# Expert down matrices issued from ScalarE's queue at the begin of their step

## The chip, the cores and the metric

The kernel runs on one core of a Trainium2 chip. The time is the device time of one execution in microseconds (us). The core's engines are TensorE (PE in the profile; its weight loads PEld), VectorE (DVE), ScalarE (ACT), GpSimd (POOL) and SyncE (SP), each with its own stream of instructions; they meet through semaphores. Transfers between memory and the on-chip buffers run on 16 DMA engines and are issued from the streams of SyncE, ScalarE and GpSimd.

## The reference

One layer of an encoder block on 512 tokens of width 1024, in float32: a projection, spatial gating and stick-breaking attention, an output product with layer norm, then a mixture of 64 routed experts (8 per token) with one shared expert, an embedding gate and a last layer norm. The change concerns the experts alone. Of the reference, this is what matters:

```python
def expert_block(args):
    tok, e = args
    xb = x_pad[tok]
    hb = jax.nn.silu(xb @ w_gate[e]) * (xb @ w_up[e])
    return hb @ w_down[e]
yb = lax.map(expert_block, ...)
routed = jax.ops.segment_sum(yb * row_w[:, None], row_tok, ...)
```

w_gate[e] and w_up[e] are 1024 x 256, w_down[e] is 256 x 1024: three matrices of 1 MB for each expert, 192 MB in all.

## The kernel before, in words

The stages follow one another: the dense part (`mix_stage`, `out_stage`), the experts (`experts_stage`), and the embedding gate with the last norm (`Embedding`). The span of the experts' loop is from about 412 to 1028 us.

All products of the experts keep float32 accuracy with three matmuls: each operand is split into a high part (rounded to fp32r by ScalarE) and a low part (the rest, by VectorE), and `product3` (lines 414 to 416) computes hi*hi, lo*hi and hi*lo. So each weight matrix that lands in a raw buffer is read once by ScalarE, which writes the high part, and once by VectorE, which writes the low part.

The work on one expert x is spread over steps. There are 64 steps, written out by hand for every engine as `step(x)`; `all_experts` unrolls the first four and the last eight, and runs the others as a hardware loop of four steps a pass. In step x:

- TensorE turns h of expert x-1 (`turn_h`, line 1532), locates the tokens of x+4 (line 1499), multiplies gate and up of x (24 matmuls of 512 columns), turns the gathered rows of x+1 (line 1508), and multiplies down of x-1 (12 matmuls).
- ScalarE copies the high part of h of x-1 (hT_hi, line 1622), the high parts of gate and up of x+1 (w_hi, line 1603, twice), between them scales the result of x-2 (y, line 1637) and writes an index list (put_idx, line 1629), then silu of x (line 1618), the high part of the rows of x+1 (xgT_hi, line 1613), and the high part of down of x (dn_hi, line 1609).
- VectorE does the low parts in the same order: hT_lo (line 1739), w_lo twice (line 1718), found and get_idx and the one-hot tiles of later experts between them, h_ff = silu * up (line 1734), xgT_lo (line 1728) and dn_lo (line 1723).
- GpSimd gathers the rows of x+4 (line 1821) and scatters those of x-1 with an add (line 1833).
- SyncE loads the weights. `load_down(x)` (line 1464) waits until VectorE has split the down matrix of x-2, which frees one of two raw buffers, dn_raw. `load_gate_up(x+2)` (line 451, once for each half) waits until the low parts of x are written, which frees one of four buffers, gu_raw. SyncE has no other work in the loop, so it runs ahead of the step that ScalarE and VectorE are in, as far as these waits let it.

The first and the last step differ. In step 0 ScalarE has only put_idx, dn_hi, silu and xgT_hi to do, dn_hi standing before silu. In the last step (`at == -1`) there is nothing left to split of gate and up, and dn_hi stands before silu on ScalarE and dn_lo before h_ff on VectorE. After its last step SyncE issues the loads of the embedding stage: p_rows (line 1906), p_w (line 1907) and two pieces of ple_raw (line 380).

Two lines carry the synchronisation of the down matrix on ScalarE:

```python
act.wait_ge(dn_in[x.b], 16 * x.turn2)          # the load has landed
act.wait_ge(y_sum, x.it - 2 + 1 + LEAD)        # the product of x-2 is done
```

Of the kernel before, what the change touches and what calls it, by code (L numbers as in the profile page):

```python
# [17 lines left out]
P = 128  # L18
# [1113 lines left out]
class Routing:  # L1132
# [32 lines left out]
    def load_down(self, sp):  # L1165
        sp.dma_start(self.m.sh_down[:], self.a["sh_w_down"][0].rearrange("(p j) n -> p (j n)", p=P)) \
          .then_inc(self.down_in, 16)
# [224 lines left out]
def experts_stage(nc, m, ps, stack, a, h1, acc_dram, acc_odd_dram, CAP, early, routing, embedding):  # L1392
# [7 lines left out]
    LEAD = 2  # L1400
# [4 lines left out]
    w_down = a["moe_w_down"][0]  # L1405
    def sem(name):
        return stack.enter_context(nc.semaphore(f"moe_{name}"))

    gu_in, put, cleared = early.gu_in, early.put, early.cleared
    dn_in = [sem(f"dn_in{b}") for b in range(2)]  # L1410
    gu_hi, gu_lo = sem("gu_hi"), sem("gu_lo")
    dn_hi, dn_lo = sem("dn_hi"), sem("dn_lo")
# [12 lines left out]
    def rounds(eng, body, finish=None):  # L1425

        eng.wait_ge(routing.peak_ready, 1)
        peak[0] = eng.value_load(m.peak_i[0:1, 0:1], min_val=0, max_val=SEQ)
        body(0, True)
        if finish is not None:  # L1430
            with eng.If(peak[0] <= CAP):
                finish(eng)
        with eng.If(peak[0] > CAP):
            with eng.Fori(1, ROUNDS) as r:
                with eng.If(peak[0] > r * CAP):
                    body(r, False)
            if finish is not None:
                finish(eng)

    def all_experts(eng, r, step):  # L1440

        for q in range(4):
            step(Expert(r, 0, q), q)
        with eng.Fori(1, QUADS - 2) as quad:
            for q in range(4):
                step(Expert(r, quad, q))
        for quad in (QUADS - 2, QUADS - 1):
            for q in range(4):
                step(Expert(r, quad, q), 4 * (quad - QUADS) + q)

    def x_banks():

        return ps[:, XT:XT + 2, 0:4 * CAP]

    def sync(sp):
        def load_gate_up(x):
            for half in range(2):

                sp.wait_ge(gu_lo, 2 * x.it + half - 4 + 1 + 2 * LEAD)
                early.load_half(sp, x, half)  # L1460

        def load_down(x):
            sp.wait_ge(dn_lo, x.it - 2 + 1 + LEAD)
            sp.dma_start(m.dn_raw[:, x.b:x.b + 1],
                         w_down[bass.ds(x.e, 1)].rearrange("o (p j) n -> p o (j n)", p=P)) \
              .then_inc(dn_in[x.b], 16)

        def body(r, first):
            if not first:
                for q in range(3):  # L1470
                    load_gate_up(Expert(r, 0, q))

            def step(x, at=99):
                load_down(x)
                if at not in (0, -1, -2):
                    load_gate_up(x.next(2))

            all_experts(sp, r, step)
            with sp.If(peak[0] <= (r + 1) * CAP):
                sp.wait_ge(gu_lo, 2 * ((r + 1) * NE) + 2 * LEAD)  # L1480
                embedding.load_p(sp)
                embedding.load_weights(sp, 0)

        load_gate_up(Expert(0, 0, 2))
        rounds(sp, body)
        embedding.sync(sp)
# [111 lines left out]
    def scalar(act):  # L1598
        def split(x, half):
            act.wait_ge(gu_in[x.b][half], 16 * x.turn2)  # L1600
            if half == 0:
                act.wait_ge(gu_sum, x.it - 2 + 1 + LEAD)
            nc.scalar.activation(m.w_hi[:, 2 * x.b + half], m.gu_raw[:, 2 * x.b + half],  # L1603
                                 ACT.Copy).then_inc(gu_hi, 1)

        def split_down(x):
            act.wait_ge(dn_in[x.b], 16 * x.turn2)
            act.wait_ge(y_sum, x.it - 2 + 1 + LEAD)
            nc.scalar.activation(m.dn_hi[:, x.b], m.dn_raw[:, x.b], ACT.Copy).then_inc(dn_hi, 1)  # L1609

        def split_x(x):
            act.wait_ge(x_turned, x.it + 1 + LEAD4)
            nc.scalar.activation(m.xgT_hi[:, x.b].rearrange("p (c n) -> p c n", c=2), x_banks(),  # L1613
                                 ACT.Copy).then_inc(x_hi, 1)

        def silu(x):
            act.wait_ge(gu_sum, x.it + 1 + LEAD)
            nc.scalar.activation(m.silu[0:CAP, x.b], ps[0:CAP, GU[x.b], 0:FF], ACT.Silu).then_inc(silu_out, 1)

        def split_hT(x):  # L1620
            act.wait_ge(h_turned, x.it + 1)
            nc.scalar.activation(m.hT_hi[:, x.b], ps[:, HT, 0:2 * CAP], ACT.Copy).then_inc(hT_hi, 1)

        def put_list(x, at=99):

            if at not in (0, 2):
                act.wait_ge(put[x.b], 16 * (x.turn2 - 2 + ZEROS[x.b]))
            act.wait_ge(found, x.it + 1 + LEAD)
            nc.scalar.activation(m.put_idx[x.q][0:CAP],  # L1629
                                 m.found[0:CAP, bass.ds(x.e, 1), 0:1].rearrange("p o c -> p (o c)"),  # L1630
                                 ACT.Identity, bias=m.far[0:CAP]).then_inc(put_ready, 1)

        def scale_y(x, bank=Y):

            act.wait_ge(y_sum, x.it + 1 + LEAD)
            act.wait_ge(put[x.b], 16 * (x.turn2 - 1 + ZEROS[x.b]))
            nc.scalar.activation(m.y[x.b][0:CAP].rearrange("p (c n) -> p c n", n=512), ps[0:CAP, bank:bank + 2],
                                 ACT.Copy,
                                 scale=m.found[0:CAP, bass.ds(x.e, 1), 1:2].rearrange("p o c -> p (o c)")) \
              .then_inc(y_ready, 1)  # L1640

        def body(r, first):
            if not first:
                for q in range(2):
                    split(Expert(r, 0, q), 0)
                    split(Expert(r, 0, q), 1)
                split_x(Expert(r, 0, 0))

            def step(x, at=99):
                if at != 0:  # L1650
                    split_hT(x.next(-1))
                if at not in (0, -1):
                    split(x.next(1), 0)
                if at not in (0, 1):
                    scale_y(x.next(-2))
                put_list(x, at if first else 99)
                if at not in (0, -1):
                    split(x.next(1), 1)
                if at in (0, -1):
                    split_down(x)  # L1660
                silu(x)
                if at != -1:
                    split_x(x.next(1))
                if at not in (0, -1):
                    split_down(x)
                if at == -1:
                    split_hT(x)
                    scale_y(x.next(-1))

            all_experts(act, r, step)  # L1670
            scale_y(Expert(r, QUADS - 1, 3), bank=XT)

        act.sem_inc(y_ready, LEAD)
        split(Expert(0, 0, 0), 0)
        routing.silu(act, 0)
        split(Expert(0, 0, 0), 1)
        routing.silu(act, 1)
        routing.sigmoid(act)
        routing.silu(act, 2)
        routing.silu(act, 3)  # L1680
        routing.copy_hT(act, 0)
        routing.copy_hT(act, 1)
        split(Expert(0, 0, 1), 0)
        split(Expert(0, 0, 1), 1)
        routing.copy_hT(act, 2)
        routing.copy_hT(act, 3)
        routing.store_rows(act, 0)
        routing.store_rows(act, 1)
        split_x(Expert(0, 0, 0))
        routing.store_rows(act, 2)  # L1690
        routing.store_rows(act, 3)
        rounds(act, body, embedding.scalar_weights)
        embedding.scalar(act)
# [119 lines left out]
    def gpsimd(pool):  # L1813
# [50 lines left out]
        embedding.gpsimd(pool)  # L1864

    return Stage(sync, tensor, scalar, vector, gpsimd, prime)


# [286 lines left out]
```

## Time and profile before

| | us |
|---|---|
| median of 3 runs | 1108.08 |
| lowest, highest | 1106.89, 1109.62 |
| profiled execution | 1109.13 |
| span of its trace | 1107.4 |
| TensorE, VectorE, ScalarE busy | 1069.6, 864.8, 713.8 |
| mean granted TensorE clock | 0.993 |

How to read it: the span is from the first to the last instruction of the core. Busy time is the time in which at least one instruction of the engine runs; a matmul's end is modelled and overlaps the next one's start, so that the distance between starts is the better measure of TensorE's rate. A row of the timeline begins with the start and the length in us; a bracket at its end gives the idle time of the engine before it and what ended it. SPq and ACTq are the sequencers of SyncE and ScalarE, which issue DMAs while the engine itself is not counted as busy. The DMA share is the time that packets took divided by 16 engines.

### The profile page before, as it was taken

What the parts mean: (1) busy time and instruction counts of PE and PEld (TensorE: products, weight loads), DVE (VectorE), ACT (ScalarE), POOL (GpSimd) and SP (SyncE); (2) the same over time, 40 slices, a digit from 0 to 9 for tenths busy, and PEclk for the clock granted to TensorE, in tenths of its full rate; (3) what the DMA queues carried; (4) which work ended last, traced back from release to release, by engine and by line L of the source; (5) the groups of instructions that cost most, each with busy time, mean ns of one, the idle gap of its engine ahead of it and who ended that gap; (6) DMA issues with size and microseconds to landing.
All of it is one profiled execution on the core that took longest, in us unless ns stands there. A gap on an engine that the chain in (4) does not pass through costs nothing.

```text
span 1107.4 us, 15674 instructions
## 1 busy us (share of the span) xinstructions
PE 1069.6 (97%) x5374; PEld 871.6 (79%) x5374; DVE 864.8 (78%) x966; ACT 713.8 (64%) x761; POOL 298.9 (27%) x173
## 2 busy tenths in 40 slices
PE   4999999999999989999999999999999999999986
PEld 3878877778888747888888888888888888888575
DVE  6654345662365687999999999999999999998366
ACT  3431235452143426888888888888888888888643
POOL 1000000000004023444444444444444444432101
PEclk9999999999999999999999999999999999999999
DMA  9432221113365357999999999999999999998811
GB/s 328 153 117 76 76 77 59 57 47 143 114 239 211 132 204 265 362 389 384 386 376 379 383 386 391 390 387 379 379 380 374 377 389 386 388 388 279 288 71 59
DMA packets 72573, 294.81 MB, mean 266 GB/s; under 512 B 15313, under 2 KB 18385, under 8 KB 47697
## 3 DMA queue, kind: packets, MB, share of 16 engines
q1 hardware_dynamic: 52944, 256.43, 59.1%
q0 software_dynamic: 19008, 35.71, 12.6%
q10 hardware_dynamic: 576, 2.10, 0.5%
q8 instruction: 26, 0.43, 0.2%
q14 instruction: 19, 0.15, 0.0%
HBM read 283.67 MB, written 44.04 MB: 296 GB/s over the span
## 4 chain that ended last, share of the span: by engine, by line
PE 88%; DVE 6%; DMA 3%; issue 1%; ACT 1%; SPq 0%; DVEq 0%; POOLq 0%; ACTq 0%
PE ps L414 26%; PE ps L416 25%; PE ps L415 25%; PE ps L1508 5%; PE ps L1532 1%; DVE w_lo L398 1%; PE ps L729 1%; PE ps L753 1%; DMA x_odd<-odd_rows 1%; PE ps L740 1%; DMA xg<-h_rows,get_idx 1%; DMA ln_b<-in_ln_in_b 1%; DVE x_rows L310 0%; PE ps L1499 0%; PE ps L323 0%
## 5 line engine op out<-in xcount | busy, mean ns | idle before, releaser
L1718 DVE TENSOR_TENSOR w_lo<-gu_raw,w_hi 128x2048 fp32r<-128x2048 f32 x128 | 292.2, 2283 | 3.3 <-ACT w_hi L1603 3.3
L1603 ACT ACTIVATE w_hi<-gu_raw 128x2048 fp32r<-128x2048 f32 x128 | 244.8, 1913 | 0.0
L414 PE MATMUL ps<-w_hi,xgT_hi 128*128 128x512 f32 x512 | 206.6, 404 | 4.1 <-issue 4.1
L416 PE MATMUL ps<-w_hi,xgT_lo 128*128 128x512 f32 x512 | 201.6, 394 | 0.0
L415 PE MATMUL ps<-w_lo,xgT_hi 128*128 128x512 f32 x512 | 200.9, 392 | 0.0
L1821 POOL DMA_INDIRECT xg<-h_rows,get_idx x64 | 143.2, 2237 | 74.8 <-DVE get_idx L1712 55.1
L414 PE MATMUL ps<-w_hi,act_hi 128*128 128x512 f32 x384 | 155.3, 404 | 5.2 <-DVE act_lo L2035 3.6
L1723 DVE TENSOR_TENSOR dn_lo<-dn_raw,dn_hi 128x2048 fp32r<-128x2048 f32 x64 | 146.7, 2292 | 8.4 <-ACT dn_hi L1609 4.8
L416 PE MATMUL ps<-w_hi,act_lo 128*128 128x512 f32 x384 | 151.4, 394 | 0.0
L415 PE MATMUL ps<-w_lo,act_hi 128*128 128x512 f32 x384 | 151.3, 394 | 0.0
L1609 ACT ACTIVATE dn_hi<-dn_raw 128x2048 fp32r<-128x2048 f32 x64 | 122.1, 1908 | 0.0
L293 POOL TENSOR_TENSOR x_rows<-x_rows,ln_b 128x1024 f32<-128x1024 f32 x6 | 14.8, 2459 | 392.0 <-DVE x_rows L286 392.0
L414 PEld LDWEIGHTS ps<-w_hi,xgT_hi 128*128 128x128 f32 x512 | 96.9, 189 | 22.8 <-issue 4.2
L416 PEld LDWEIGHTS ps<-w_hi,xgT_lo 128*128 128x128 f32 x512 | 96.9, 189 | 20.9
L415 PEld LDWEIGHTS ps<-w_lo,xgT_hi 128*128 128x128 f32 x512 | 97.1, 190 | 18.5
L1833 POOL DMA_INDIRECT residual_rows<-y,put_idx x32 | 64.6, 2018 | 162.8 <-ACT put_idx L1629 88.8
L414 PE MATMUL ps<-dn_hi,hT_hi 128*128 128x512 f32 x256 | 105.4, 412 | 0.0
L1833 POOL DMA_INDIRECT odd_rows<-y,put_idx x32 | 62.6, 1957 | 157.9 <-ACT put_idx L1629 156.7
L416 PE MATMUL ps<-dn_hi,hT_lo 128*128 128x512 f32 x256 | 101.0, 395 | 0.0
L415 PE MATMUL ps<-dn_lo,hT_hi 128*128 128x512 f32 x256 | 100.2, 391 | 0.0
L393 ACT ACTIVATE w_hi<-raw 128x2048 fp32r<-128x2048 f32 x28 | 53.4, 1915 | 64.0 <-PE ps L416 48.1
L1613 ACT ACTIVATE xgT_hi<-ps 128x1024 fp32r<-128x1024 f32 x64 | 65.8, 1029 | 41.3 <-PE ps L1508 41.3
(198 smaller groups left out, 1738.3 us busy)
## 6 DMA issues: line engine op xcount, KB each, us to landing
gu_raw<-in_moe_w_gate SPq DMA_DIRECT2D x64, 1024.0 KB, 10.1
gu_raw<-in_moe_w_up SPq DMA_DIRECT2D x64, 1024.0 KB, 9.9
dn_raw<-in_moe_w_down SPq DMA_DIRECT2D x64, 1024.0 KB, 9.1
raw<-in_w_in SPq DMA_DIRECT2D x18, 1024.0 KB, 5.1
h_rows<-x_rows SPq DMA_DIRECT2D x8, 512.0 KB, 5.0
raw<-in_w_out SPq DMA_DIRECT2D x4, 1024.0 KB, 5.0
ple_raw<-in_ple_w_gate SPq DMA_DIRECT2D x4, 1024.0 KB, 10.9
x_rows<-in_x SPq DMA_DIRECT2D x4, 512.0 KB, 9.9
```

The lines of the kernel that those rows point to most:

```text
L393: self.nc.scalar.activation(self.m.w_hi[:, i % NSPLIT], self.raw[i % self.slots], ACT.Copy).then_inc(self.hi_split, 1)
L414: nc.tensor.matmul(out, x_hi, w_hi, start=first, stop=False)
L415: nc.tensor.matmul(out, x_hi, w_lo, start=False, stop=False)
L416: return nc.tensor.matmul(out, x_lo, w_hi, start=False, stop=last)
L1508: last = nc.tensor.transpose(ps[:, XT + k // 4, (k % 4) * CAP:(k % 4 + 1) * CAP], m.xg[x.q][0:CAP, k::KD], m.ident[0:CAP, 0:CAP])
L1603: nc.scalar.activation(m.w_hi[:, 2 * x.b + half], m.gu_raw[:, 2 * x.b + half], ACT.Copy).then_inc(gu_hi, 1)
L1609: nc.scalar.activation(m.dn_hi[:, x.b], m.dn_raw[:, x.b], ACT.Copy).then_inc(dn_hi, 1)
L1613: nc.scalar.activation(m.xgT_hi[:, x.b].rearrange("p (c n) -> p c n", c=2), x_banks(), ACT.Copy).then_inc(x_hi, 1)
L1718: nc.vector.tensor_tensor(m.w_lo[:, 2 * x.b + half], m.gu_raw[:, 2 * x.b + half], m.w_hi[:, 2 * x.b + half].bitcast(F32), ALU.subtract).th ...
L1723: nc.vector.tensor_tensor(m.dn_lo[:, x.b], m.dn_raw[:, x.b], m.dn_hi[:, x.b].bitcast(F32), ALU.subtract).then_inc(dn_lo, 1)
L1821: nc.gpsimd.indirect_dma_start(out=m.xg[x.q][0:CAP], out_offset=None, in_=h1, in_offset=bass.IndirectOffsetOnAxis(ap=m.get_idx[x.q][0:CAP] ...
L1833: nc.gpsimd.indirect_dma_start(out=(acc_dram, acc_odd_dram)[x.b], out_offset=bass.IndirectOffsetOnAxis(ap=m.put_idx[x.q][0:CAP], axis=0), ...
```

## The change

The function `load_down` moves from SyncE's stream to ScalarE's, with the same wait, the same transfer and the same semaphores. SyncE's step is left with the gate and up loads. On ScalarE the load stands at the begin of step x, behind hT_hi of x-1 and before the first split of gate and up of x+1.

```diff
-        def load_down(x):
-            sp.wait_ge(dn_lo, x.it - 2 + 1 + LEAD)
-            sp.dma_start(m.dn_raw[:, x.b:x.b + 1],
-                         w_down[bass.ds(x.e, 1)].rearrange("o (p j) n -> p o (j n)", p=P)) \
-              .then_inc(dn_in[x.b], 16)
-
...
             def step(x, at=99):
-                load_down(x)
                 if at not in (0, -1, -2):
                     load_gate_up(x.next(2))
...
+        def load_down(x):
+            act.wait_ge(dn_lo, x.it - 2 + 1 + LEAD)
+            act.dma_start(m.dn_raw[:, x.b:x.b + 1],
+                          w_down[bass.ds(x.e, 1)].rearrange("o (p j) n -> p o (j n)", p=P)) \
+               .then_inc(dn_in[x.b], 16)
+
...
             def step(x, at=99):
                 if at != 0:
                     split_hT(x.next(-1))
+                load_down(x)
                 if at not in (0, -1):
                     split(x.next(1), 0)
```

ScalarE, an unrolled step (x = 3) of the kernel before; dn_raw is the raw down matrix, dn_hi its high part, w_hi that of gate or up, ps is PSUM:

```order
L1622 ACTIVATE hT_hi<-ps 128x256 [waits moe_h_turned]
L1603 ACTIVATE w_hi<-gu_raw 128x2048 [waits moe_gu_sum,moe_gu_in00]
L1637 ACTIVATE y_138<-ps,found 128x1024 [waits moe_put_odd,moe_y_sum]
L1629 ACTIVATE put_idx_122<-found,far 128x1 [waits moe_found,moe_put_odd]
L1603 ACTIVATE w_hi<-gu_raw 128x2048 [waits moe_gu_in01]
L1618 ACTIVATE silu<-ps 128x256 [waits moe_gu_sum]
L1613 ACTIVATE xgT_hi<-ps 128x1024 [waits moe_x_turned]
L1609 ACTIVATE dn_hi<-dn_raw 128x2048 [waits moe_y_sum,moe_dn_in1]
```

The same step of the changed kernel (its line numbers from here on are lower by one on ScalarE and by seven above it):

```order
L1621 ACTIVATE hT_hi<-ps 128x256 [waits moe_h_turned]
L1601 DMA dn_raw<-in_moe_w_down 128x2048 [waits moe_dn_lo]
L1596 ACTIVATE w_hi<-gu_raw 128x2048 [waits moe_gu_sum,moe_gu_in00]
L1636 ACTIVATE y_138<-ps,found 128x1024 [waits moe_put_odd,moe_y_sum]
L1628 ACTIVATE put_idx_122<-found,far 128x1 [waits moe_found,moe_put_odd]
L1596 ACTIVATE w_hi<-gu_raw 128x2048 [waits moe_gu_in01]
L1617 ACTIVATE silu<-ps 128x256 [waits moe_gu_sum]
L1612 ACTIVATE xgT_hi<-ps 128x1024 [waits moe_x_turned]
L1608 ACTIVATE dn_hi<-dn_raw 128x2048 [waits moe_y_sum,moe_dn_in1]
```

The load stands seven instructions ahead of the dn_hi that reads it, both in one step.

ScalarE at the begin of the loop, step 0, in the changed kernel:

```order
L1428 TENSOR_LOAD peak_i [waits route_peak_ready]
L1428 ISA x2
L1601 DMA dn_raw<-in_moe_w_down 128x2048 [waits moe_dn_lo]
L1628 ACTIVATE put_idx_119<-found,far 128x1 [waits moe_found]
L1608 ACTIVATE dn_hi<-dn_raw 128x2048 [waits moe_y_sum,moe_dn_in0]
L1617 ACTIVATE silu<-ps 128x256 [waits moe_gu_sum]
L1612 ACTIVATE xgT_hi<-ps 128x1024 [waits moe_x_turned]
```

Only put_idx stands between the load and its reader, and silu and xgT_hi stand behind the reader.

ScalarE in the last step, in the changed kernel:

```order
L1621 ACTIVATE hT_hi<-ps 128x256 [waits moe_h_turned]
L1601 DMA dn_raw<-in_moe_w_down 128x2048 [waits moe_dn_lo]
L1636 ACTIVATE y_138<-ps,found 128x1024 [waits moe_put_odd,moe_y_sum]
L1628 ACTIVATE put_idx_122<-found,far 128x1 [waits moe_found,moe_put_odd]
L1608 ACTIVATE dn_hi<-dn_raw 128x2048 [waits moe_y_sum,moe_dn_in1]
L1617 ACTIVATE silu<-ps 128x256 [waits moe_gu_sum]
```

Here y and put_idx stand between the load and its reader.

## Rows read from the trace of the kernel before

**Rows 1.** The page: engines' busy time, and DMA busy tenths in 40 slices.
```profile
PE 1069.6 (97%) x5374; PEld 871.6 (79%) x5374; DVE 864.8 (78%) x966; ACT 713.8 (64%) x761; POOL 298.9 (27%) x173
...
DMA  9432221113365357999999999999999999998811
```

**Rows 2.** Windows: PE, PEld, DVE, ACT, POOL busy (x), PEclk, DMA share, GB/s.
```profile
600.00:650.00 50.00, 50.00 (x261) 42.19 (x261) 48.98 (x49) 44.04 (x43) 22.92 (x11) 1.00 1.02 386
```

**Rows 3.** Timeline of ScalarE in one step: start, us, engine, line, operation.
```profile
702.10 0.39 ACT L1622 ACTIVATE hT_hi<-ps 128x256 fp32r<-128x256 f32 x1 [0.17 <-PE ps L1532]
702.38 1.91 ACT L1603 ACTIVATE w_hi<-gu_raw 128x2048 fp32r<-128x2048 f32 x1
...
707.78 0.38 ACT L1618 ACTIVATE silu<-ps 128x256 f32<-128x256 f32 x1 [0.50 <-PE ps L416]
...
709.60 1.91 ACT L1609 ACTIVATE dn_hi<-dn_raw 128x2048 fp32r<-128x2048 f32 x1
```

**Rows 4.** Timeline of SyncE in the same step.
```profile
700.39 0.33 SPq L451 DMA_DIRECT2D gu_raw<-in_moe_w_up  x1
704.28 0.33 SPq L1464 DMA_DIRECT2D dn_raw<-in_moe_w_down  x1
```

**Rows 5.** Timeline of TensorE and VectorE in the same step and the next's begin.
```profile
702.00 0.48 PE L414 MATMUL ps<-w_hi,xgT_hi 128*128 128x512 f32 x1
...
704.51 2.28 DVE L1718 TENSOR_TENSOR w_lo<-gu_raw,w_hi 128x2048 fp32r<-128x2048 f32 x1
...
710.15 1.22 DVE L1728 TENSOR_TENSOR xgT_lo<-ps,xgT_hi 128x1024 fp32r<-128x1024 f32 x1
...
711.54 2.29 DVE L1723 TENSOR_TENSOR dn_lo<-dn_raw,dn_hi 128x2048 fp32r<-128x2048 f32 x1 [0.17 <-ACT dn_hi L1609]
...
711.58 0.47 PE L414 MATMUL ps<-w_hi,xgT_hi 128*128 128x512 f32 x1
```

**Rows 6.** Line 1464: landings of the down loads issued at 425, 465, 580, 963.
```profile
DMA to landing us min/median/max: 4.7/4.7/4.7
...
DMA to landing us min/median/max: 8.1/8.1/8.1
...
DMA to landing us min/median/max: 6.5/6.5/6.5
...
DMA to landing us min/median/max: 12.6/12.6/12.6
```

**Rows 7.** Line 1821: landings of gathers issued at 413, 560 to 580, 950 to 980.
```profile
DMA to landing us min/median/max: 4.5/4.5/4.5
...
DMA to landing us min/median/max: 10.3/10.4/10.5
...
DMA to landing us min/median/max: 10.5/11.0/12.4
```

**Rows 8.** Begin of the loop: ScalarE's timeline, and TensorE's waits (us, times, longest).
```profile
415.74 1.90 ACT L1609 ACTIVATE dn_hi<-dn_raw 128x2048 fp32r<-128x2048 f32 x1
419.78 0.39 ACT L1618 ACTIVATE silu<-ps 128x256 f32<-128x256 f32 x1 [2.15 <-PE ps L416]
420.66 1.02 ACT L1613 ACTIVATE xgT_hi<-ps 128x1024 fp32r<-128x1024 f32 x1 [0.49 <-PE ps L1508]
...
PE ps L414 <- issue: 4.1, 2, 2.3
...
PE ps L1508 <- DMA xg<-h_rows,get_idx: 0.5, 1, 0.5
```

**Rows 9.** End of the loop: timelines of ScalarE, VectorE and SyncE.
```profile
1017.08 0.39 ACT L1622 ACTIVATE hT_hi<-ps 128x256 fp32r<-128x256 f32 x1 [0.17 <-PE ps L1532]
...
1020.49 2.29 DVE L1723 TENSOR_TENSOR dn_lo<-dn_raw,dn_hi 128x2048 fp32r<-128x2048 f32 x1 [0.91 <-ACT dn_hi L1609]
1022.98 0.42 DVE L1734 TENSOR_TENSOR h_ff<-silu,ps 128x256 f32<-128x256 f32 x1 [0.20 <-ACT silu L1618]
...
1015.25 0.38 SPq L1906 DMA_DIRECT2D p_rows<-in_p  x1
```

## The prediction

> **What bounds the kernel now.** I read the page first. TensorE is busy for 97% of the span and VectorE for 78%; the row of the DMA engines shows nines from the fifteenth slice to the thirty-eighth, and that stretch is the experts' stage [rows 1]. Ask next what a window inside it shows: in 50 us TensorE is busy for 50.00, VectorE for 48.98, ScalarE for 44.04, and the DMA share is 1.02 [rows 2]. So three things are full at once there: the matmuls, VectorE and the DMA engines. The timeline of one step says what the period is: the first gate/up matmul stands at 702.00 and the next step's at 711.58, 9.58 us a step without a gap between [rows 5]. Nothing that becomes earlier can shorten such a step; anything that becomes later by more than its slack lengthens it. The reader is to look, then, for slack on three chains: ScalarE to VectorE to TensorE within a step, the landing of the down matrix, and the two ends of the loop, where steps look different.
>
> **What moves.** SyncE issued the down load of expert x as soon as VectorE had split that of x-2, which is nearly a step ahead: the issue at 704.28 [rows 4] is for the next step's expert, whose conversion on ScalarE comes 9.58 us after the one at 709.60 [rows 3], at about 719.2. That is 14.9 us of time to land. Now ScalarE issues it behind hT_hi of its own step (702.10, [rows 3]), so at about 702.3, and the conversion of the same expert is at 709.60. That leaves 7.3 us. The load is the same 1 MB; SyncE's queue loses a third of its loads.
>
> **Term 1, the begin of the loop.** In step 0 the issue stands directly ahead of put_idx and dn_hi. Before, dn_hi ran at 415.74 since its data had long landed [rows 8]. Now the load starts at about 415.4, ahead of put_idx, which takes some 0.3. A down load with idle engines took 4.7 us, and one with other loads about it took 8.1 [rows 6]; here one more gate/up load and two gathers are under way, and I take 6.2, so it lands at 421.6. dn_hi then ends at 423.5 (1.91 us each). Behind it in ScalarE's order stand silu (0.39 us, before at 419.78) and xgT_hi (before at 420.66), and TensorE's second step waits for the latter by way of VectorE [rows 8]. xgT_hi now starts at about 423.8, 3.1 us late. On the other side two loads of 1 MB are gone from ahead of the first gather, but TensorE waited only 0.5 us for that gather [rows 8], so no more than 0.5 comes back. The term is +2.6; with 4.7 it is +1.1, with 8.1 it is +4.5.
>
> **Term 2, the end of the loop.** In the last step dn_hi stands ahead of silu, since no gate/up split is left. The load is issued behind hT_hi at 1017.08, at about 1017.2, and SyncE has put four loads of the next stage in front from 1015.25 on, on the other queue [rows 9]. With 4.7 us it lands at 1021.9, with 8.1 at 1025.3; I take 6.8 and 1024.0. Then come dn_hi (1.91) and on VectorE dn_lo (2.29), which stands ahead of h_ff. Before, dn_lo was through by 1022.78 and h_ff ran at 1022.98, released by silu [rows 9]. Now h_ff can't start before 1024.0 + 1.91 + 2.29 = 1028.2. That is +5.2, and turning h, the down product, the scatter and the next stage all follow from it, so it goes to the end in full. The ends are +3.1 and +6.5.
>
> **Term 3, the issue itself.** SyncE's issue took 0.33 us [rows 4]; with the address arithmetic I take 0.4 on ScalarE. It stands between hT_hi and the first w_hi (702.38), so that w_hi ends at 704.69 instead of 704.29 and w_lo, at 704.51 before, starts at 704.72: +0.2. From w_lo on VectorE runs without a gap to xgT_lo, which ends at 711.37, against TensorE's start at 711.58 [rows 5]. So 0.2 of slack meets 0.2 of delay: I count 0.05 for each of 60 steps, 3 us. ScalarE has the room (0.50 idle before silu [rows 3]), so the second w_hi's delay is nearly covered, and dn_hi isn't moved at all. If the issue were hidden wholly in the shadow of hT_hi the cost is 0; if all 0.4 shows behind the slack, it is 0.2 a step, 12 us.
>
> **Term 4, landing within 7.3 us.** Landing times of the down loads rise from 4.7 on idle engines to 8.1 at 465, fall to 6.5 at 580, and rise to 12.6 at 963 [rows 6]. That is a queue filling slowly: the DMA engines need a trace more than a step for a step's bytes, and the 14.9 us of slack pay for it. With 7.3 us they can't. Put the new slack in the old queue's terms: a load issued at 704.28 that must be there at 709.60 may take 5.3. If the engines are the limit from there on, all of 12.6 - 5.3 = 7.3 us must be spent in waiting somewhere in the loop, once, not in each step, because every wait lets the queue drain. A step that is already longer by term 3 drains it as well, so the two don't add up: 7.3 with 3 beside it I count as 9 together, the ends being 0 and 48 (below). VectorE has 0.17 idle before dn_lo [rows 5], so a late dn_hi reaches TensorE almost whole.
>
> The nearest rows for a load on another queue are the gathers of GpSimd's: 4.5 us on idle engines, 10.4 at 565, 11.0 at 950 to 980 [rows 7], while the loads of SyncE's queue went from 6.5 to 12.6. So a queue beside the full one pays some 6 us for the company, but it doesn't stand behind the whole backlog. A gather's time includes GpSimd's own work on it, so I take it as an upper bound for the down load.
>
> **The rule on this.** The Trainium skill ("DMA: Bandwidth & Descriptors", section "Queues, rings and completion order") says that each DMA engine goes round the queues that have work and drains one packet of descriptors from one before it turns to the next. By that rule a down load on its own queue would wait for what is being served and no more, and the loop would cost nothing; the gathers' level times agree with it. This is the second rival. The section "Issuing engines are not separate DMA queues" of that page says that all issuers share the same 16 engines, which speaks against any gain in bandwidth; the share of 1.02 agrees.
>
> **The sum.** 2.6 + 5.2 + 9 = 16.8 us. The profiled execution took 1109.13 (span 1107.4), 1.05 over the median of the runs shown, 1108.08. 1108.08 + 16.8 = 1124.9; I say 1125.
>
> **The rivals.**
> - *The load is late in every step.* Each landing takes about the 8.1 of row 465 although the queue drains, because ScalarE's load always meets the second gate/up half, issued at 700.39, 1.9 us before it [rows 4], and the gathers. Then 0.8 us in each of 60 steps, 48 us, with terms 1 and 2: 1108 + 56 = 1164. For it: the 8.1 and the gathers' 10.4. Against it: 6.5 at 580 under the same load, and a longer step makes room, which brings the landing towards 4.7. 15%, from 1133 to 1165.
> - *The load is hidden in the loop.* Served beside the backlog it lands in under 7.3 us; what is left is terms 1 to 3: 1108 + 7.8 + 0 to 3 = 1117. For it: the gathers' times don't follow the backlog. Against it: their level is high. 20%, from 1112 to 1120.
> - *Faster.* The first gather and the first steps gain from the lighter queue while the waits at both ends are covered. TensorE's idle time there is 0.5 before the first gather's transposes and 4.1 before the first matmuls of the first two steps [rows 8], so the most it gives is 4.6: 1103.5. It decides only if the loads of steps 0 and 63 land before their conversions are due, 0.3 us and 1.3 us after the issue, where 4.7 is the shortest seen. 4%.
> - *No difference.* Terms 1 and 2 at their lower ends (4.2 us) less what other idle time swallows: 5%.
>
> The forecast itself, all three terms with waits that spend the backlog once, has 56%, with 1120 to 1133 as its own range. Another mean clock is an uncertainty upward: TensorE's granted clock was 0.993 over the span, so part of it ran at the lower level, and longer pauses at the ends may add to that; I don't price it. Below 1112 I leave 9% and above 1146 some 9%. What a measurement of this kernel can tell from no change is about 0.3%, 3.3 us. Slower by more than that: 56 + 15 + 20 = 91%; within it 5%; faster 4%.
>
> **What would show it.** In the new trace dn_hi of step 0 should start near 421.6 and idle time on ScalarE before it should be put down to the load; in the last step dn_hi should stand some 5 us late and h_ff behind it. In the loop, ScalarE's first w_hi should start about 0.7 behind hT_hi instead of 0.28. Waits of dn_hi for the load should appear in many steps, small (0.1 to 1 us) and in sum 5 to 10 us, with landings of down loads near 7.3, and the DMA share still at 1. No waits in the loop would mean the second rival; waits of equal size in all steps and a DMA share clearly under 1 the first. I am wrong if the sum over the two ends is under 4 us, or if TensorE's period in the middle is still 9.58 with the down load landing late, which would mean slack on VectorE that I haven't seen.

## The result, and the profile after

| | before | after |
|---|---|---|
| median, us | 1108.36 (1106.89 to 1109.62, 4 runs) | 1180.96 (1178.98 to 1182.84, 4 runs) |
| ratio | | 1.0655, 95% interval 1.0632 to 1.0678 |
| span of the profiled execution, us | 1107.4 | 1181.1 |
| granted clock over the span | 0.993 | 0.984 |

The kernel is 6.5% slower. The forecast was 1125 us with a range up to 1146: the sign was right, the size four times too small. I place the difference first by the starts of the gate/up matmuls of each step on TensorE (line 414, before and after), which cut the span into four pieces:

| piece | before, us | after, us | change | forecast |
|---|---|---|---|---|
| up to the first step's matmuls | 412.41 | 411.30 | -1.1 | -0.5 at most |
| first step | 10.63 | 16.80 | +6.2 | +3.1 |
| all further steps | 593.8 | 655.2 | +61.5 | +9 |
| from the last step's start to the end | 90.6 | 97.76 | +7.15 | +5.2 |

The four add up to 73.7, which is the difference of the spans. Five sixths of it lie in the loop, where the mean step went from 9.58 us to 10.57. The first two pieces belong together: the second step begins 5.1 us later (423.04, 428.10), and the 1.1 us by which the first begins earlier are waited again.

A part of the loop's cost stands beside a lower clock. TensorE's granted clock was 0.986 on average over the further steps, 0.997 before: four stretches of 3.4 us at the lower level (from 545, 757, 928 and 1033) are new, in a stretch where TensorE now pauses in most steps. They account for at most some 7 us of the 61.5 (1.4% of 655.2 less 0.3% of 593.8); how much of that the waits below cover no run tells.

The page of the new kernel answers to [rows 1]: busy shares, the DMA engines' busy tenths in 40 slices, the queues (packets, MB, share of 16 engines' time), the chain that ended last, and two groups of instructions with the idle time ahead of them.
```profile
PE 1100.9 (93%) x5374; PEld 881.2 (75%) x5374; DVE 866.6 (73%) x966; ACT 709.3 (60%) x761; POOL 312.2 (26%) x173
...
DMA  8422303043463369999999999999999999998631
...
q1 hardware_dynamic: 43728, 189.32, 44.4%
q10 hardware_dynamic: 9792, 69.21, 14.1%
...
DMA 44%; PE 41%; DVE 7%; issue 3%; ACT 3%; SPq 0%; ACTq 0%; DVEq 0%; POOLq 0%
...
L1723 DVE TENSOR_TENSOR dn_lo<-dn_raw,dn_hi 128x2048 fp32r<-128x2048 f32 x64 | 146.7, 2292 | 73.5 <-ACT dn_hi L1608 73.3
L1608 ACT ACTIVATE dn_hi<-dn_raw 128x2048 fp32r<-128x2048 f32 x64 | 122.5, 1914 | 115.8 <-DMA dn_raw<-in_moe_w_down 113.7
```
The down loads have a queue of their own now (q10). The chain that ended last goes through DMA for 44% of the span, and the wait of dn_hi for its load is 113.7 us; VectorE passes it on as 73.3 us ahead of dn_lo. The number of instructions is the same on every engine.

The windows answer to [rows 2] (busy of PE, PEld, DVE, ACT, POOL; PEclk, DMA share, GB/s).
```profile
600.00:650.00 50.00, 47.59 (x240) 38.79 (x239) 45.02 (x45) 38.79 (x39) 22.92 (x10) 1.00 0.99 353
700.00:750.00 50.00, 47.53 (x235) 38.41 (x234) 43.46 (x42) 38.39 (x38) 20.45 (x9) 1.00 1.00 350
```
TensorE has gaps of 2.4 us in 50, in two windows at a full clock. The DMA share has hardly moved (1.02 before), but what the engines move fell from 386 to 350 GB/s.

ScalarE's timeline over two steps answers to [rows 3] (start, us, engine, line, operation, in brackets the idle time before it).
```profile
712.47 1.91 ACT L1608 ACTIVATE dn_hi<-dn_raw 128x2048 fp32r<-128x2048 f32 x1 [2.16 <-DMA dn_raw<-in_moe_w_down]
713.12 0.34 ACTq L1601 DMA_DIRECT2D dn_raw<-in_moe_w_down  x1
714.29 0.37 ACT L1621 ACTIVATE hT_hi<-ps 128x256 fp32r<-128x256 f32 x1
714.55 1.91 ACT L1596 ACTIVATE w_hi<-gu_raw 128x2048 fp32r<-128x2048 f32 x1
...
719.35 0.38 ACT L1617 ACTIVATE silu<-ps 128x256 f32<-128x256 f32 x1
720.11 1.03 ACT L1612 ACTIVATE xgT_hi<-ps 128x1024 fp32r<-128x1024 f32 x1 [0.39 <-PE ps L1501]
723.69 1.92 ACT L1608 ACTIVATE dn_hi<-dn_raw 128x2048 fp32r<-128x2048 f32 x1 [2.55 <-DMA dn_raw<-in_moe_w_down]
```
The conversion at 723.69 starts when its load lands, 2.55 us after xgT_hi. That load was issued at 713.12, while the conversion before it still ran and ahead of hT_hi at 714.29: ScalarE's queue hands a DMA issue on while the engine computes. What the issue follows is the wait of hT_hi, which stands ahead of it in the program: TensorE must have turned h (line 1525). Three rows of ScalarE and TensorE two steps on show it:
```profile
733.38 1.91 ACT L1608 ACTIVATE dn_hi<-dn_raw 128x2048 fp32r<-128x2048 f32 x1 [1.53 <-DMA dn_raw<-in_moe_w_down]
733.95 0.50 PE L1525 MATMUL ps<-ident,h_ff 128*128 128x128 f32 x2 [0.49 <-DVE h_ff L1734]
734.62 0.34 ACTq L1601 DMA_DIRECT2D dn_raw<-in_moe_w_down  x1
```
The issue comes 0.17 us after the turn's end at 734.45. In steps 1 to 62 it does so within 0.3 us in 53 cases; in 6 of the other 9, where h was turned before, it comes 0.14 us after the begin of the conversion. Where no conversion waits (half_down below), the issue comes 2.2 us after the begin of the conversion before it, and 7.4 to 7.5 us are left to its own: the lead that I had forecast. Here the conversions are late themselves, so the issue comes only 0.8 us after the begin of the one before, on average over loads issued from 450 to 980. The landing takes 9.7 us, and the two make a step of 10.6.

SyncE's timeline answers to [rows 4], VectorE's to [rows 5].
```profile
711.89 0.33 SPq L451 DMA_DIRECT2D gu_raw<-in_moe_w_up  x1
719.42 0.33 SPq L451 DMA_DIRECT2D gu_raw<-in_moe_w_gate  x1
```
```profile
714.42 2.29 DVE L1723 TENSOR_TENSOR dn_lo<-dn_raw,dn_hi 128x2048 fp32r<-128x2048 f32 x1 [1.09 <-ACT dn_hi L1608]
```
The up half goes out 1.23 us ahead of the down load and is being served when that arrives.

The begin of the loop answers to [rows 8].
```profile
413.83 0.65 ACTq L1601 DMA_DIRECT2D dn_raw<-in_moe_w_down  x1
...
423.65 1.91 ACT L1608 ACTIVATE dn_hi<-dn_raw 128x2048 fp32r<-128x2048 f32 x1 [8.83 <-DMA dn_raw<-in_moe_w_down]
...
425.73 1.02 ACT L1612 ACTIVATE xgT_hi<-ps 128x1024 fp32r<-128x1024 f32 x1
```
The end of the loop answers to [rows 9], ScalarE ahead of VectorE.
```profile
1082.80 0.40 ACTq L1601 DMA_DIRECT2D dn_raw<-in_moe_w_down  x1
...
1092.57 1.91 ACT L1608 ACTIVATE dn_hi<-dn_raw 128x2048 fp32r<-128x2048 f32 x1 [7.97 <-DMA dn_raw<-in_moe_w_down]
```
```profile
1094.51 2.29 DVE L1723 TENSOR_TENSOR dn_lo<-dn_raw,dn_hi 128x2048 fp32r<-128x2048 f32 x1 [8.73 <-ACT dn_hi L1608]
1096.72 0.41 DVE L1734 TENSOR_TENSOR h_ff<-silu,ps 128x256 f32<-128x256 f32 x1
```
From issue to conversion it is 9.8 us in the first step and 9.8 in the last, where I had taken 6.2 and 6.8.

The waits between 400 and 1100 (total us, times, longest).
```profile
ACT dn_hi L1608 <- DMA dn_raw<-in_moe_w_down: 113.7, 56, 8.8
...
DVE dn_lo L1723 <- ACT dn_hi L1608: 73.3, 56, 8.7
...
PE ps L1525 <- DVE h_ff L1734: 22.1, 27, 6.8
...
PE ps L414 <- DVE xgT_lo L1728: 12.0, 40, 0.4
```
Dn_hi waits in 56 of 64 steps. Without the two ends (8.8 and 8.0) 96.9 us are left in 54 steps, 1.8 each. ScalarE was idle for some 1.1 us a step before (44.04 busy of 50 in [rows 2]), and a part of the wait takes the place of that idle time: the steps grew by 1.0 and not by 1.8.

### The profile page after: what moved, and what is told of

Read it like the earlier page. It is cut to its first block, busy times and chain, and to the rows that moved or that the text cites. A ratio compares the mean times of both kernels' runs of the same rounds, so it can differ in the third digit from the quotient of the medians.

```text
span 1181.1 us, 15689 instructions
## 1 busy us (share of the span) xinstructions
PE 1100.9 (93%) x5374; PEld 881.2 (75%) x5374; DVE 866.6 (73%) x966; ACT 709.3 (60%) x761; POOL 312.2 (26%) x173
## 3 DMA queue, kind: packets, MB, share of 16 engines
q0 software_dynamic: 19008, 35.71, 12.4%
HBM read 283.67 MB, written 44.04 MB: 277 GB/s over the span
## 4 chain that ended last, share of the span: by engine, by line
DMA 44%; PE 41%; DVE 7%; issue 3%; ACT 3%; SPq 0%; ACTq 0%; DVEq 0%; POOLq 0%
DMA dn_raw<-in_moe_w_down 42%; PE ps L414 12%; PE ps L416 11%; PE ps L415 11%; ACT dn_hi L1608 2%; DVE w_lo L1718 2%; DVE w_lo L398 1%; PE ps L729 1%; PE ps L753 1%; PE ps L740 1%; DMA x_odd<-odd_rows 1%; PE ps L1248 1%; PE ps L1501 1%; DMA ln_b<-in_ln_in_b 1%; DVE dn_lo L1723 0%
## 5 line engine op out<-in xcount | busy, mean ns | idle before, releaser
L414 PE MATMUL ps<-w_hi,xgT_hi 128*128 128x512 f32 x512 | 210.5, 411 | 17.9 <-DVE xgT_lo L1728 12.0
L416 PE MATMUL ps<-w_hi,xgT_lo 128*128 128x512 f32 x512 | 204.2, 399 | 0.0
L415 PE MATMUL ps<-w_lo,xgT_hi 128*128 128x512 f32 x512 | 203.6, 398 | 0.0
L1723 DVE TENSOR_TENSOR dn_lo<-dn_raw,dn_hi 128x2048 fp32r<-128x2048 f32 x64 | 146.7, 2292 | 73.5 <-ACT dn_hi L1608 73.3
L1608 ACT ACTIVATE dn_hi<-dn_raw 128x2048 fp32r<-128x2048 f32 x64 | 122.5, 1914 | 115.8 <-DMA dn_raw<-in_moe_w_down 113.7
L1833 POOL DMA_INDIRECT odd_rows<-y,put_idx x32 | 69.6, 2175 | 193.9 <-ACT put_idx L1628 192.1
L1833 POOL DMA_INDIRECT residual_rows<-y,put_idx x32 | 72.2, 2256 | 183.0 <-ACT put_idx L1628 100.0
L414 PEld LDWEIGHTS ps<-w_hi,act_hi 128*128 128x128 f32 x384 | 72.7, 189 | 20.5 <-issue 4.2
## 6 DMA issues: line engine op xcount, KB each, us to landing
ple_raw<-in_ple_w_gate SPq DMA_DIRECT2D x4, 1024.0 KB, 12.4
```

The costliest lines, as they stand in the source:

```text
L414: nc.tensor.matmul(out, x_hi, w_hi, start=first, stop=False)
L415: nc.tensor.matmul(out, x_hi, w_lo, start=False, stop=False)
L416: return nc.tensor.matmul(out, x_lo, w_hi, start=False, stop=last)
L1723: nc.vector.tensor_tensor(m.dn_lo[:, x.b], m.dn_raw[:, x.b], m.dn_hi[:, x.b].bitcast(F32), ALU.subtract).then_inc(dn_lo, 1)
L1833: nc.gpsimd.indirect_dma_start(out=(acc_dram, acc_odd_dram)[x.b], out_offset=bass.IndirectOffsetOnAxis(ap=m.put_idx[x.q][0:CAP], axis=0), ...
```

## The experiments

The question was which of four things costs the 61 us of the loop: that the load has a queue of its own, that ScalarE issues it, that it has less time, or that the DMA engines have too much to do. Each run is compared with runs of the kernel before on the same chip.

**lead_put** keeps the second queue and the issuing engine, but gives back the time: in step x ScalarE issues the load of x+1, behind put_idx; SyncE does it for the first two.
```diff
-                load_down(x)
...
                 put_list(x, at if first else 99)
+                if at not in (0, -1):
+                    load_down(x.next(1))
```


> ScalarE still issues the down loads, but that of expert x+1 in step x, behind put_idx; SyncE issues those of steps 0 and 1 as before. Theory A (the lead: each load is issued only once the conversion of the one before it has begun, so a step can't be shorter than a landing of 9.9 us and 0.7): with some 14 us of lead the loop is back at 9.57 us a step and the time at 1108, within 4 us. Theory B (two queues: the DMA engines move 350 instead of 385 GB/s when SyncE's and ScalarE's loads run side by side, and a step is as long as that takes): the loop stays at 10.6 us a step, 1168. Theory C (the issue on ScalarE costs 0.4 us a step): 1108 + 24 = 1132.

Measured: 1109.54 us against 1109.31, ratio 1.0005 (0.9995 to 1.0015). The issue, the conversion of the expert before, and a window:
```profile
702.74 0.34 ACTq L1609 DMA_DIRECT2D dn_raw<-in_moe_w_down  x1
...
707.87 1.91 ACT L1616 ACTIVATE dn_hi<-dn_raw 128x2048 fp32r<-128x2048 f32 x1
```
```profile
700.00:750.00 50.00, 50.00 (x265) 42.29 (x264) 48.97 (x47) 44.04 (x43) 21.56 (x10) 1.00 1.03 384
```
The issue comes 5.1 us ahead of the conversion of the expert before and so a step more, 14.7, ahead of its own. The window is that of the kernel before [rows 2]. So the second queue and the issue on ScalarE, at this place, cost nothing. What costs is the lead.

**lead_splitx** is the same with the issue later by some 4 us, just ahead of the conversion of x.
```diff
+                if at not in (0, -1):
+                    load_down(x.next(1))
                 if at not in (0, -1):
                     split_down(x)
```


> As the one with the load behind put_idx, but the load of x+1 is issued in step x just ahead of the conversion of x, so one whole step ahead of its own conversion and before the wait for its predecessor. Theory A: a landing of 9 to 10 us against a step of 9.57, so waits of 0 to 0.5 us: 1108 to 1135. Theory B: 1168, as with the other place. If it isn't the lead but that only one load can be in flight, it is at 1108 to 1112.

Measured: 1130.9 us, ratio 1.0204 (1.0166 to 1.0241). The lead is 10.3 to 12.4 us, 11.2 on average.
```profile
700.00:750.00 50.00, 48.71 (x250) 40.46 (x248) 46.77 (x46) 43.18 (x43) 22.95 (x10) 1.00 1.00 370
```
```profile
ACT dn_hi L1616 <- DMA dn_raw<-in_moe_w_down: 22.9, 27, 1.9
```
The wait (here between 450 and 980) is back in half of the steps, and the mean step is 9.90 us. The loop costs a third of what it does in the changed kernel. With no wait the lead would be a step and the 0.8 us by which the issue is ahead of the conversion before, 10.4 us, against landings of 10.9 on average; in the changed kernel it would be 7.4 against 9.7. So the loads are late by some 0.6 us here and by 2.3 there, and 0.3 and 1.0 us a step of it reach TensorE.

**ends_on_sync** is the changed kernel with the loads of the first and the last step back on SyncE.
```diff
+                if at in (0, -1):
+                    load_down(x)
                 if at not in (0, -1, -2):
                     load_gate_up(x.next(2))
...
                     split_hT(x.next(-1))
-                load_down(x)
+                if at not in (0, -1):
+                    load_down(x)
```


> The changed kernel, but SyncE issues the down loads of step 0 and step 63 where it did before; ScalarE the 62 others at the begin of their own step. The traces say that the begin of the loop costs 6.2 us and the end 7.2: expected 1181 - 13 = 1168. If the ends' waits are covered by other work, it stays at 1181; if the begin also sets the state in which the queues go through the loop, it falls by more.

Measured: 1166.03 us, ratio 1.0509 (1.0476 to 1.0541).
```profile
700.00:750.00 50.00, 47.30 (x238) 38.44 (x238) 45.14 (x45) 38.38 (x39) 23.07 (x10) 1.00 0.99 349
```
```profile
ACT dn_hi L1616 <- DMA dn_raw<-in_moe_w_down: 98.1, 54, 3.4
```
By the same pieces as above it stands to the kernel before at -0.3, -1.6, +61.3 and -1.1 us; the -1.6 is a first step at a granted clock of 0.99 instead of 0.84. All of the 15.4 us by which its span is shorter than the changed kernel's come from the ends, and the 61.3 beside the 61.5 there say that the cost of the loop doesn't depend on how it begins.

**sync_late2** tests the queue by itself: the kernel before, with one queue, but SyncE issues the down load behind the gate/up halves of two steps on, and only once hT_hi of the step before is written.
```diff
-            sp.wait_ge(dn_lo, x.it - 2 + 1 + LEAD)
...
+                sp.wait_ge(hT_hi, x.it)
...
-                load_down(x)
                 if at not in (0, -1, -2):
                     load_gate_up(x.next(2))
+                load_down(x)
```


> SyncE issues all loads, in one queue, but the down load of x only when ScalarE has written hT_hi of x-1, behind the gate and up loads of x+2. Theory A (the lead alone): the load stands behind one gate/up half in its own queue and lands in 6.5 to 8.5 us; a step is landing + 2.4 us, 9.6 to 10.9, so 1120 to 1195. Theory B (two queues side by side are the cost): with one queue the loop is at 9.6 to 9.8, 1121 to 1135, the ends included.

Measured: 1171.4 us, ratio 1.0561 (1.0543 to 1.0578). The window, the wait over 450 to 980, and the landings of loads issued from 600 to 700:
```profile
700.00:750.00 50.00, 47.27 (x240) 39.08 (x238) 45.05 (x45) 39.39 (x39) 22.38 (x10) 1.00 0.99 362
```
```profile
ACT dn_hi L1612 <- DMA dn_raw<-in_moe_w_down: 75.5, 42, 4.1
```
```profile
DMA to landing us min/median/max: 6.7/7.6/11.2
```
A late load in the old queue costs nearly what the change costs: the loop is 65.9 us longer than before. This isn't a clean copy. The load stands behind gate/up loads of its own queue; its issue waits until hT_hi is written, which stands behind the conversion in ScalarE's order, so that here a late landing delays the next issue in full (issue 2.3 us after the begin of the conversion, landing 8.3, a step of 10.6); and the granted clock over the loop is 0.977, so up to some 14 us of the 65.9 stand beside the lower level. But it shows that a second queue isn't needed for the loss.

The next four runs keep the changed kernel's late issue and take away traffic. **half_gate_up** loads 512 KB instead of 1 MB of each gate and up matrix from the fifth expert on (the rest of the tile keeps old numbers).
```diff
-        sp.dma_start(self.m.gu_raw[:, 2 * x.b + half:2 * x.b + half + 1], rows).then_inc(self.gu_in[x.b][half], 16)
...
+            sp.dma_start(self.m.gu_raw[:, 2 * x.b + half:2 * x.b + half + 1, 0:HC // 2],
+                         rows[:, :, 0:HC // 2]).then_inc(self.gu_in[x.b][half], 16)
```


> The changed kernel with only the first half of each row of the gate and up matrices loaded from expert 4 on (512 KB instead of 1 MB each; the other half of the buffer keeps old values). It asks what the 9.9 us of a down load's landing consist of. Theory D (company: on each DMA engine packets of SyncE's queue go in turn with those of the down load, eight against eight): the landing falls by half of the company's time and by the shorter start, to 6 to 7 us, the loop is at 9.57 a step, and the time is 1108 + 13 for the two ends = 1121. Theory E (the landing is ruled by the gathers and scatters of GpSimd's queue): it stays over 9 us and the time over 1165.

Measured: 1130.21 us against 1108.68, ratio 1.0200 (1.0159 to 1.0241).
```profile
700.00:750.00 50.00, 49.79 (x261) 41.98 (x260) 48.81 (x46) 43.75 (x42) 22.18 (x12) 1.00 0.94 272
```
```profile
ACT w_hi L1600 <- issue: 14.3, 48, 0.4
...
ACT dn_hi L1612 <- DMA dn_raw<-in_moe_w_down: 2.4, 6, 0.7
```
With a third of the weights' bytes gone the wait for the load is gone (450 to 980), and landings are 7.3 us at the median of the loads issued from 600 to 700. In its place stands a small one of w_hi, 0.3 us in 48 steps: it is the issue between hT_hi and w_hi, which in the changed kernel hides in dn_hi's wait.

**few_rows** gathers and scatters 16 rows for each expert instead of 128.
```diff
-            nc.gpsimd.indirect_dma_start(out=m.xg[x.q][0:CAP], ...
+            nc.gpsimd.indirect_dma_start(out=m.xg[x.q][0:16], ...
...
-                                         in_=m.y[x.b][0:CAP], ...
+                                         in_=m.y[x.b][0:16], ...
```


> The changed kernel with gathers and scatters of 16 rows instead of up to 128 (the other rows keep old values and aren't added), all weight loads whole. Theory D: the landing of a down load still has the gate and up packets beside it and falls by about 1 to 2 us only, to 8 to 9, a step to 9.6 to 9.9: 1125 to 1145. Theory E: it falls below 7 us and the time to 1121.

Measured: 1126.18 us, ratio 1.0164 (1.0127 to 1.0200).
```profile
700.00:750.00 50.00, 49.85 (x260) 42.03 (x259) 48.99 (x48) 44.27 (x41) 21.19 (x11) 1.00 0.92 335
```
```profile
ACT dn_hi L1608 <- DMA dn_raw<-in_moe_w_down: 1.7, 2, 1.2
```

**half_down** loads 512 KB of each down matrix from the third expert on; the rest of the tile keeps old numbers.
```diff
-            act.dma_start(m.dn_raw[:, x.b:x.b + 1],
...
+                act.dma_start(m.dn_raw[:, x.b:x.b + 1, 0:HC // 2], rows[:, :, 0:HC // 2]).then_inc(dn_in[x.b], 16)
```


> The changed kernel with only the first half of each row of the down matrix loaded from expert 2 on (512 KB), at the begin of its own step as in the changed kernel. Theory D: the time to the first packet (3.5 us) and the completion (0.9) stay and the middle part of 5.3 us halves: 7.1 us, so hardly a wait in the loop: 1115 to 1130 with the ends. If the landing is mostly time before the first packet, it stays above 8.5 us and 1140.

Measured: 1129.31 us, ratio 1.0204 (1.0160 to 1.0248).
```profile
ACT dn_hi L1610 <- DMA dn_raw<-in_moe_w_down: 1.9, 4, 0.6
```
Three different cuts give the same end, 18 to 23 us over the kernel before, and hardly a wait for the load in the loop. Landings of loads issued from 450 to 980 fall from 9.7 us to 7.2 (half_gate_up), 6.4 (few_rows) and 6.5 (half_down), each under its lead of 7.5. None of the three streams is the culprit by itself: the load shares the engines with both others, and less of any one brings it in under its lead. What is left is the ends and the issue.

**lead_silu** adds a point between lead_put and lead_splitx: the load of x+1 behind silu of x.
```diff
                 silu(x)
+                if at not in (0, -1):
+                    load_down(x.next(1))
```

> As the version with the load of x+1 behind put_idx, but behind silu in step x: the lead is 11.4 us instead of 14.8. Theory A: landings of 10 to 11 us fit in, the loop is at 9.57 to 9.65 a step: 1108 to 1114. If landings on the second queue are longer than 12 us once nothing waits, 1115 to 1130.

Measured: 1116.25 us, ratio 1.0086 (1.0052 to 1.0120); lead 11.3 us.
```profile
ACT dn_hi L1616 <- DMA dn_raw<-in_moe_w_down: 5.8, 9, 1.5
```
Landings are 11.0 us on average here and 9.5 in lead_put. So 14.7 us of lead cost nothing, 11.3 cost 0.9%, and one step or little more 2.0%.

**few_rows_ends** joins few_rows and ends_on_sync: nothing should be left but the issue.

> Gathers and scatters of 16 rows (the others keep old values and aren't added), and SyncE issues the down loads of steps 0 and 63 as before; so neither the ends nor late landings in the loop should cost anything, and the issue on ScalarE behind hT_hi is left alone. Expected from the version with 16 rows (9.64 us a step, ScalarE's first w_hi late by 0.3 in most steps): 60 x 0.09 = 5 us, so 1113. If the 5 us come from the late landings after all: 1108. If the ends cost more than their 13 us: below 1110.

Measured: 1109.87 us against 1108.89, ratio 1.0012 (0.9999 to 1.0025). I had expected some 1113.
```profile
ACT w_hi L1604 <- issue: 15.5, 52, 0.4
```
The total misleads here. From the first step's matmuls to the last's it is 610.2 us, 5.8 more than the 604.4 before, and from there to the end 86.05 instead of 90.6. ends_on_sync, with whole scatters, took 89.5 there, so some 3.5 us go with the smaller scatters, in part by a higher granted clock (0.966 instead of 0.958). The 5.8 us are the issue between hT_hi and w_hi: ScalarE has no wait for the load left in the loop, and in lead_put, with the issue behind put_idx, the same stretch is 0.3 us over before. It isn't even: one step in four, that into a new pass of the hardware loop, is 9.88 us instead of 9.61, the others longer by 0.03 to 0.07.

**most_down** asks how the cost sets in: half_down with 768 KB.
```diff
-                act.dma_start(m.dn_raw[:, x.b:x.b + 1, 0:HC // 2], rows[:, :, 0:HC // 2])
+                act.dma_start(m.dn_raw[:, x.b:x.b + 1, 0:3 * HC // 4], rows[:, :, 0:3 * HC // 4])
```


> The changed kernel with three quarters of each row of the down matrix loaded from expert 2 on (768 KB). Theory D (the step is the landing and 0.65 us, since the next load is issued once the conversion has begun; a landing is 3.5 us to the first packet, eight turns of 0.62 to 0.66 and 0.9): with six turns 8.3 to 8.7 us, a step of 9.65 ruled by the issue alone, 1128. Theory F (the DMA engines are the limit: with short queues a packet of 8 KB takes 0.355 us and not 0.318, 24 of them and 2.0 for rows are 10.5 us a step): 22 packets are 9.8 us a step, 1108 + 20 + 60 x 0.2 = 1140.

Measured: 1154.16 us, ratio 1.0419 (1.0393 to 1.0445).
```profile
700.00:750.00 50.00, 49.26 (x255) 41.00 (x254) 47.40 (x46) 41.24 (x41) 22.07 (x11) 1.00 0.99 342
```
```profile
ACT dn_hi L1610 <- DMA dn_raw<-in_moe_w_down: 38.9, 39, 2.3
```
Both theories had less. The first to the last step take 639.3 us, 34.9 over before, half of what the full load costs; most steps lie between 9.55 and 10.7 us, the longest in the loop is 11.9. There is no sharp point at which the wait sets in: between 450 and 980 it goes 1.9, 38.9 and (in the changed kernel) 84.5 us for 512, 768 and 1024 KB.

## Why the prediction was wrong

**The failed step is term 4.** It said that all of 7.3 us must be waited "once, not in each step, because every wait lets the queue drain". The wait came in nearly every step, and the loop became 61.5 us longer where terms 3 and 4 together had 9. Two things were wrong in it.

First, the model of one queue whose backlog is spent. The lead without a wait was right, 7.4 to 7.5 us where a run shows it. What was wrong is that landings would come down to it. Over the loads issued from 450 to 980 a landing took 9.2 us on average before (6.4 to 12.6), 9.5 in lead_put and 9.7 in the changed kernel, where it doesn't fall along the loop: 9.6 at 459, 10.4 at 681, 9.6 at 979. So the landings are much as before, and each load is late anew by some 2.3 us, of which 1.0 us a step reaches TensorE.

What a landing consists of the packets show. In each step the load is issued 1.2 us behind an up half (the median), meets it and the gather and scatter, and shares the engines with them. Of the packets of 50 such loads the first is served 3.5 us after the issue, the middle one after 6.0. Between a load's first and its 32nd packet 30 packets of 8 KB of SyncE's queue start on average, so the two are served about one to one. The three cuts bear this out: the middle packet comes at 4.0 with 16 rows, 4.4 with half the gate/up bytes, 4.8 with half the down bytes. This company is there anew in each step, however long the step before was. The gather's 10.4 us beside a full queue [rows 7] was the nearest row for a load on another queue and had the right size; I had set it aside as an upper bound because a part of it is GpSimd's own work. The fall from 8.1 to 6.5 in [rows 6], which I took as proof of draining, didn't last: in the kernel before each of the loads issued from 695 to 1001 took 9.1 us or more.

Second, the drain itself gives less than I counted. The engines don't catch up in a longer step, they move less in it: 350 GB/s against 386 at a share of 1. The queues over 600 to 700 show it (packets, MB, share of 16 engines' 100 us), before:
```profile
GB/s 431 421 356 384 423 406 334 392 413 393 344 415 385 351 338 411 395 388 311 421 418 359 334 416 429 359 329 415 429 354 384 421 423 325 393 424 395 339 420 415
...
q1 hardware_dynamic: 4517, 32.88, 80.0%
```
and after:
```profile
GB/s 421 372 272 244 410 413 370 326 400 402 316 288 343 410 316 295 307 419 395 341 295 410 400 341 287 416 385 269 279 388 423 243 279 339 421 383 321 295 385 416
...
q1 hardware_dynamic: 2678, 19.51, 54.1%
q10 hardware_dynamic: 1413, 10.36, 24.6%
```
In slices of 2.5 us the lowest rate falls from 311 to 243 GB/s, though the engines count as busy throughout. A packet of SyncE's queue takes 0.800 × 1600 / 4517 = 283 ns before and 0.541 × 1600 / 2678 = 323 after. Lower GB/s alone would only restate the longer step, since the bytes of a step are the same; that the share stays near 1 is what makes a step of 10.6 us look as full as one of 9.6.

**Terms 1 and 2, the ends.** The mechanism was as forecast, to the chain from dn_hi over silu to xgT_hi and over dn_lo to h_ff. The size of both was off, by the same number: 9.8 us from issue to conversion instead of 6.2 and 6.8. The landings I took them from, 4.7 to 8.1 [rows 6], were of loads in SyncE's own queue. In step 0 an error the other way hid a part: the issue came at 413.83, not at 415.4. So xgT_hi is 5.1 us late (425.73) where I had 3.1. The first step does begin 1.1 us earlier, more than the 0.5 I had allowed, but xgT_hi sets the second step and takes it back: 5.1 us were measured for term 1's 2.6. At the end +7.15 was measured for 5.2; the granted clock there was 0.942 instead of 0.958, which is at most 1.8 us of it.

**Term 3, the issue.** 3 us forecast, 5.8 measured where it shows (few_rows_ends). In the changed kernel it doesn't: w_hi waits for issue for 1.1 us in all, since the issue goes out during dn_hi.

**The rivals.** The one that was right in kind was "late in every step", at 15%: landing set by the up half and the gathers. It gave 1164 and a range up to 1165, with 0.8 us a step; measured are 1.0 a step, and 12 us for the ends instead of 8. "Hidden in the loop" is refuted for this load, though it is served beside the others' backlog as that rival said: sharing the engines with two other streams, a load of 1 MB takes longer than alone, 9.7 us against 4.7. I had read "doesn't wait for the backlog" as "lands early". That two queues bring no bandwidth held: lead_put moved 384 GB/s, the kernel before 386.

**The marks I had named.** Dn_hi of step 0 was to start near 421.6: 423.65. Small waits summing to 5 to 10: 96.9. Landings near 7.3: 9.7. A DMA share clearly under 1 was to mark the rival that came true; it stayed at 0.99 and 1.00 in the two windows, so that mark was worthless (below). The lower clock that I had named and not priced is at most some 9 us, 7 in the loop and 2 at the end.

**What stays open.** Why packets take longer when the queues are shorter. The runs show it with one queue (362 GB/s in sync_late2) and with two, so it isn't the second queue; whether it is a cause of the late landings or goes with them, none of these runs tells. Also open is what the four low stretches of the clock cost, and why 2.3 us of lateness make a step longer by 1.0 and not by more or less; only that ScalarE and VectorE had idle time to lose can be read.

## What to carry to other kernels

When a load moves to another issuer, compare leads, not queues: the time from issue to first use, against a landing taken from a row with the same company, for a load that shares the engines with another queue (here 9.7 us for 1 MB, twice that of a load alone). If the issue is tied to the begin of its own step, and the lead that this leaves is shorter than a landing, the loss repeats in each step instead of being spent once. Issuing one step ahead from the same engine (lead_put) costs nothing and keeps the old time.

## What the runs showed of the hardware

- A DMA share near 1 isn't a measure of throughput: with a third of the bytes gone (half_gate_up) the share was still 0.94 at 272 GB/s, with few_rows 0.92 at 335, and 1.02 at 386 in the kernel before.
- ScalarE's queue hands on a DMA issue behind an operation that still waits for the engine: the issue at 713.12 lies in dn_hi's 712.47 to 714.38, though hT_hi, at 714.29, stands ahead of it in the program. It does wait for what that operation waits for: in 53 of 62 steps it came within 0.3 us of the end of TensorE's turn of h, hT_hi's input (0.17 at 734.62).
- An issue of 0.34 us on ScalarE shows as some 0.3 us ahead of the next operation and costs about 0.1 us a step here (few_rows_ends), the rest being slack.
